# Weight sums on VectorE, a tap and roundings on ScalarE, and stored split weights for the short MLP

## The chip, the core and the metric

The kernel runs on one core of one Trainium2 chip. The metric is the device time of one execution in microseconds.

## The reference

One encoder layer is applied to two sequences with shared weights: `x_sample` (1024 positions, the long one, done first) and `x_prompt` (512, the short one). D_MODEL is 1024, D_FF 3072. Only the second half of the layer matters here:

```python
mix = (sigmoid(gate_lru) * y_lru + sigmoid(gate_attn) * y_attn) @ w_o + b_o
x = layer_norm(ALPHA * x + mix, ln1_g, ln1_b)
hu = depthwise_conv(x @ w_up + b_up, w_ffn_conv, b_ffn_conv, (1, 1))
val, gt = split(hu, 2)
ffn = (gelu(gt) * val) @ w_down + b_down
return layer_norm(ALPHA * x + ffn, ln2_g, ln2_b)
```

Before it stand a projection, a bidirectional gated recurrence (RG-LRU) and a windowed attention. All is float32.

## The kernel before, in words

**Split products.** Every matrix product is made of float32r pieces: a value is rounded to a head, and the tail is the value less the head. Head x head, head x tail and tail x head are summed, so a product takes three matmuls per tile. For weights, the head is a copy (`tensor_scalar` by 1, or a ScalarE copy) into an F32R tile and the tail a `tensor_tensor` subtraction.

**Order.** Phases are `lru`, `attn` (with its output projections `y_lru`, `y_attn`, `w_o`) and `mlp`, first for the long sequence (q = 0), then for the short one (q = 1). In `lru` to `w_o` of the long sequence GpSimd splits each weight slab (L939, L940), SyncE (SP) stores the split slab in the DRAM array `w_split` (L715), and the short sequence reads it back (`fetch`, L718 to L721). The MLP's weights were not stored: the short sequence loaded them raw (`short_slab`, L912 on) and GpSimd split them again (`split_short`, L1099, the rounding L1106 and the subtraction L1107).

**Engines.** Each engine runs its own written-out list of instructions in order, tied to the others by semaphores whose counts are constants or, in loops, register values (`Fori`, `order.loop`). `order(...)` and `tell(...)` on VectorE make every instruction wait for the one before it.

**Long MLP, up.** A feature tile p (128 of 3072) has a value row and a gate row of 1024 positions, `lv_raw` and `lg_raw`. Two tiles (PLAIN) are computed plainly, with split slabs `plain`. The other 22 (FAST) are computed as pairs of 2x2 block products in Winograd's form: seven products instead of eight, `form_product` (L1533), 12 matmuls of 128x512 each. The weight side needs three plain blocks A11, A12, A22 and four sums S1 to S4, each as head and tail of 128x512 (`forms`). GpSimd makes the sums (`pair_forms`: L1036, L1038, L1043, L1044) and all seven tails (L1050), ScalarE the heads (`round_plain_forms` L2078, `round_sums` L2083). The products go in the order A11, S2, S1, A12, S3, S4, A22 into three PSUM banks of `FORM_BANKS[side]`; a bank is taken by VectorE between two products into it: `gate_second` (L2626) before S3, `value_second` (L2632) before S4, the value half of `second_halves` (L2639) before A22, the gate half (L2641) after it, and `value_first` (L2619) when the pair is done. ScalarE takes two more (`first_product` L2090, `gate_half` L2097).

The depthwise convolution of tile p = j + 1 runs beside pair j: for the gate, ScalarE does the centre tap with the bias (`centre`, L2063) and VectorE the two outer ones (L2591, L2594), then ScalarE the gelu (L2068); for the value VectorE does all three (L2599, L2601, L2603). `hidden` (L2611) multiplies them to `l_h`, which SP stores in `h_dram` (`store_h`). A raw pair of slabs is loaded by `load_pair` on SP once `form_done` says that the former pair's tiles are read (L820).

**Long MLP, down.** 48 steps: 24 k-tiles for four token tiles, then the same 24 for the other four. A step has 24 matmuls (L1588). Per step SP loads a raw slab of `w_down` (128x1024) and a half row of `h_dram` (128x512); GpSimd splits the slab (`down_slab`, L1075, L1076) into one of four ring slots `W_down`, and VectorE splits the hidden tile (`split_down_h`, L2655, L2656). Beside it VectorE prepares the residual (`start_long_sum`, L2663, L2665), and ScalarE issues the loads of `acc_down` (4 MB), of the next x (2 MB) and of five row vectors. After each half, `last_sum` and the layer norm of its token tiles run on VectorE and ScalarE.

**Short MLP.** Six groups of 12 slabs: eight up slabs (four pairs of value and gate tiles) and four down slabs, 24 matmuls each. ScalarE takes the up results from PSUM (L2158), VectorE does six taps, the product with the gelu, the cast and the tail (L2553 to L2566), and TensorE then runs the down slabs (L1483). The 12 slabs rotate over five buffers:

```python
UP_SLOT = (4, 0, 1, 2, 3, 4, 1, 4)
DOWN_SLOT = (0, 2, 3, 1)
```

so slab 7 goes where slab 5 was, and slab 2 where slab 11 of the group before was.

## Time and profile before

| | |
|---|---|
| median of three runs | 2790.64 us (2790.28 to 2797.62) |
| the profiled execution | 2797.58 us |
| its span, first to last instruction | 2795.8 us |
| mean granted TensorE clock | 0.974 |
| TensorE busy | 2642.1 us (95%) |
| VectorE busy | 1710.3 us (61%) |
| GpSimd busy | 1259.0 us (45%) |
| ScalarE busy | 848.8 us (30%) |
| DMA | 452.77 MB, mean 162 GB/s |
| chain that ended last | TensorE 62%, VectorE 16%, GpSimd 12%, ScalarE 4%, DMA 3% |

The span is the time between the first and the last instruction of the one execution that was profiled, and some 1.8 us of its time lie around it. The shares are of the span. The chain is followed back from the last instruction, at each step to what released it; an engine with a large share there held the others up. In rows of a timeline, brackets name the idle time before an instruction and what ended it.

### The profile page before, as it was taken

Reading aid. Unit: us, or ns where it says so; the run is one execution under the profiler, and the core shown is the slowest. Engines: PE = TensorE matmul, PEld = TensorE weight load, DVE = VectorE, ACT = ScalarE, POOL = GpSimd, SP = SyncE. Lnnn points to the kernel's source line nnn. Section 1 sums busy time; section 2 is a strip of 40 time slices with the busy share of each in tenths; the row PEclk is TensorE's granted clock in tenths of the full one; section 3 lists DMA queues with packets and bytes.
Section 4 is the critical chain, followed back from the end, with each engine's and each line's share of the span. In section 5 each row is a group of like instructions: output and inputs, shape, how many; then the busy total and the mean of one; then the engine's idle time right before and its main releaser. Section 6 shows DMA issues by size and latency. Waiting matters only on the chain.

```text
span 2795.8 us, 33187 instructions
## 1 busy us (share of the span) xinstructions
PE 2642.1 (95%) x11634; PEld 2166.8 (78%) x11634; DVE 1710.3 (61%) x1883; ACT 848.8 (30%) x1224; POOL 1259.0 (45%) x680
## 2 busy tenths in 40 slices
PE   8998999999899999999999798999999898899997
...
GB/s 220 194 189 160 205 172 143 192 158 159 246 341 241 284 92 46 87 71 82 75 81 129 219 137 152 169 211 226 217 222 196 330 238 76 79 87 90 90 88 85
DMA packets 155869, 452.77 MB, mean 162 GB/s; under 512 B 13895, under 2 KB 40775, under 8 KB 153712
## 3 DMA queue, kind: packets, MB, share of 16 engines
...
## 4 chain that ended last, share of the span: by engine, by line
PE 62%; DVE 16%; POOL 12%; ACT 4%; DMA 3%; issue 2%; ACTq 0%; SPq 0%; POOLq 0%; DVEq 0%
PE ps L1139 31%; PE ps L1309 8%; PE ps L1588 7%; POOL S L1050 6%; PE ps L1403 4%; POOL A L1050 3%; PE ps L1191 3%; PE ps L1483 2%; PE ps L1292 2%; PE ps L1342 1%; POOL S_sum L1036 1%; DMA gate_in<-gate_dram 1%; DVE HL L2566 1%; PE ps L1329 1%; PE ps L1194 1%
## 5 line engine op out<-in xcount | busy, mean ns | idle before, releaser
L1139 PE MATMUL ps<-XH,W 128*128 128x512 f32 x2752 | 811.3, 393 | 24.4 <-DVE XL L2244 11.9
L1139 PEld LDWEIGHTS ps<-XH,W 128*128 128x128 f32 x2752 | 519.8, 189 | 141.3 <-issue 17.7
L1139 PE MATMUL ps<-XL,W 128*128 128x512 f32 x1376 | 484.6, 392 | 0.0
L1106 POOL TENSOR_SCALAR W<-raw 128x1024 fp32r<-128x1024 f32 x72 | 83.3, 1157 | 677.7 <-PE ps L1403 502.7
L939 POOL TENSOR_SCALAR W<-raw 128x1024 fp32r<-128x1024 f32 (+2 forms) x72 | 91.8, 1275 | 567.2 <-PE ps L1139 301.8
L1139 PEld LDWEIGHTS ps<-XL,W 128*128 128x128 f32 x1376 | 260.6, 189 | 54.2
L1588 PE MATMUL ps<-Wd,Hd 128*128 128x512 f32 x1152 | 271.9, 399 | 26.7 <-DVE Hd L2656 23.5
L1588 PEld LDWEIGHTS ps<-Wd,Hd 128*128 128x128 f32 x1152 | 222.3, 194 | 76.2 <-issue 20.1
L1309 PE MATMUL ps<-XH,W 128*128 128x512 f32 x672 | 216.4, 393 | 0.0
L940 POOL TENSOR_TENSOR W<-raw,W 128x1024 fp32r<-128x1024 f32 (+2 forms) x72 | 206.5, 2868 | 6.0
L1533 PE MATMUL ps<-XH,A 128*128 128x512 f32 x528 | 173.4, 396 | 16.7 <-DVE lv_raw L2639 13.1
L1107 POOL TENSOR_TENSOR W<-raw,W 128x1024 fp32r<-128x1024 f32 x72 | 183.9, 2555 | 6.0
L1050 POOL TENSOR_TENSOR S<-S_sum,S 128x512 fp32r<-128x512 f32 x88 | 174.3, 1981 | 13.8 <-POOL S L1050 9.5
L1309 PEld LDWEIGHTS ps<-XH,W 128*128 128x128 f32 x672 | 126.2, 188 | 25.5
L1483 PE MATMUL ps<-W,HH 128*128 128x512 f32 x384 | 115.2, 420 | 28.7 <-DVE HL L2566 16.5
L1533 PEld LDWEIGHTS ps<-XH,A 128*128 128x128 f32 x528 | 99.9, 189 | 45.6 <-DVE lv_raw L2639 19.9
L1309 PE MATMUL ps<-XL,W 128*128 128x512 f32 x336 | 131.1, 390 | 0.0
L1076 POOL TENSOR_TENSOR Wd<-raw,Wd 128x1024 fp32r<-128x1024 f32 x48 | 124.9, 2603 | 4.0
L2655 DVE CAST Hd<-Hd 128x512 fp32r<-128x512 f32 x48 | 50.0, 1041 | 109.1 <-DMA Hd<-h_dram 108.1
L1483 PEld LDWEIGHTS ps<-W,HH 128*128 128x128 f32 x384 | 78.1, 205 | 48.3 <-ACT v_raw L2158 12.7
L1050 POOL TENSOR_TENSOR A<-raw,A 128x512 fp32r<-128x512 f32 x66 | 104.1, 1577 | 10.8 <-POOL A L1050 6.3
L1139 PE MATMUL ps<-ATH,W 128*128 128x512 f32 x384 | 108.2, 389 | 0.0
...
## 6 DMA issues: line engine op xcount, KB each, us to landing
w_split<-W SPq DMA_DIRECT2D x59, 1024.0 KB, 6.0
W<-w_split SPq DMA_DIRECT2D x58, 1024.0 KB, 5.6
...
```

The source lines that it names most:

```text
L939: order(pool.tensor_scalar(half(0, slot, 0)[:, 0:width], raw[slot][:, 0:width], 1.0, 1.0, ALU.mult, ALU.mult))
L940: return pool.tensor_tensor(half(0, slot, 1)[:, 0:width], raw[slot][:, 0:width], half(0, slot, 0)[:, 0:width].bitcast(F32), ALU.subtract)
L1050: pool.tensor_tensor(F[n][:, 1, :], src, F[n][:, 0, :].bitcast(F32), ALU.subtract).then_inc(form_done, 1)
L1076: pool.tensor_tensor(tail, raw[k % 2][:, 0:D_MODEL], head.bitcast(F32), ALU.subtract).then_inc(wd_split, 1)
L1107: pool.tensor_tensor(tail, raw[n % 2][:, 0:D_MODEL], head.bitcast(F32), ALU.subtract).then_inc(short_split, 1)
L1139: last = nc.tensor.matmul(bank(group, c), lhs(wl, k), rhs(xl, k, c), start=(k == 0 and n == 0), stop=(k == nk - 1 and n == 2))
L1191: nc.tensor.matmul(ps[:, first + c, :], w[wl][:, m * P:(m + 1) * P], ut[xl][:, c * CH:(c + 1) * CH], start=(i == 0), stop=False)
L1309: last = nc.tensor.matmul(ps[:, 2 + side, :], half(q, slot_of(q, "attn", slab), wl)[:, k * P:(k + 1) * P], x_rhs(xl, k, c), start=(k == 0 ...
L1403: last = nc.tensor.matmul(ps[:, 2 * pair + f, :], X[q][xl][:, k, tt * P:(tt + 1) * P], half(q, slot_of(q, "w_o", k), wl)[:, f * CH:(f + 1) ...
L1483: last = nc.tensor.matmul(ps[:, 2 * pair + f, :], (HH, HL)[xl][:, kk, tt * P:(tt + 1) * P], half(q, DOWN_SLOT[kk], wl)[:, f * CH:(f + 1) * ...
L1533: last = nc.tensor.matmul(ps[:, bank_no, :], forms[side][form][:, wl, k * P:(k + 1) * P], x_form(of, xl)[:, k, :], start=(start and k == 0 ...
L1588: last = nc.tensor.matmul(ps[:, first + f, :], H_down[slot][:, xl, (tt % 4) * P:(tt % 4 + 1) * P], W_down[slot][:, wl, f * CH:(f + 1) * CH ...
```

## The change

- **Weight sums and their tails.** S1 to S4 and their four tails are made by VectorE (`first_sums`, `last_sums`, `split_sums`), spread over its `pair_period`. GpSimd keeps the tails of A11, A12 and A22 (`split_plain_forms`).
- **A tap.** The value's centre tap with the bias goes to ScalarE (`value_centre`); VectorE keeps two value taps.
- **Down.** ScalarE rounds the weight slab and the hidden tile (`round_step`), VectorE subtracts both (`split_step`), one signal `step_split` for the two. `start_long_sum` is spread, one token tile a step, over steps 8 to 15.
- **Stores.** SP stores the split plain slabs, the three split plain forms of each pair (three times 512 KB) and, in the first half of down, each split `w_down` slab (1 MB). The fourth block A21 was never split for the long sequence: in the down-phase SP loads it raw (`rest_raw`, 256 KB), GpSimd splits it, SP stores it (512 KB), 22 times. Ring slots and forms wait for their stores.
- **Short MLP.** SP fetches split slabs (1 MB) straight into the five buffers; GpSimd does nothing there.

The core of the diff:

```diff
+                def save_forms(j, side, slab):
+
+                    sp.wait_ge(a_split, 3 * j + 3)
+                    for n in PLAIN_TILES:
+                        at = slice(0, CH) if n[2] == "1" else slice(CH, 2 * CH)
+                        sp.dma_start(w_split[slab + (n[1] == "1"), :, :, at],
+                                     forms[side][n][:, :, :].bitcast(F32)).then_inc(form_saved[side][0], 16)
+
+                def next_pair(j, side, slab):
+                    save_forms(j - 1, side, slab)
+                    sp.wait_ge(form_added, 4 * j)
                     load_pair(j + PLAIN)
                     store_h(j - 1)
...
+                def save_down(kk, slot, slab):
+                    sp.wait_ge(step_split, kk + 1)
+                    sp.dma_start(w_split[slab, :, :, 0:D_MODEL], W_down[slot][:, :, :].bitcast(F32)).then_inc(w_saved[slot], 16)
+
+                def load_rest(i, slab, k):
+                    sp.dma_start(rest_raw[k][:, :], A["w_up"][slab, :, 0:CH]).then_inc(rest_in[k][0], 16)
+
+                def save_rest(i, slab, k):
+                    sp.wait_ge(rest_split, i + 1)
+                    sp.dma_start(w_split[slab, :, :, 0:CH], rest[k][:, :, :].bitcast(F32)).then_inc(rest_saved[k][0], 16)
...
+                for kk in range(RING, FT):
+                    next_step(kk, kk, 0, kk % RING)
+                    save_down(kk - RING, kk % RING, down_slab(kk - RING))
+                    i = kk - RING
+                    if i >= 2:
+                        sp.wait_ge(rest_split, i - 1)
+                    load_rest(i, 2 * (PLAIN + i), i % 2)
+                    if i:
+                        save_rest(i - 1, up_slab(PLAIN + i - 1, 0), (i - 1) % 2)
...
-                    sp.wait_ge(out_stored[k], 16 * out_count(0)[k])
+                s0 = first_slab(1, "mlp")
                 for n in range(12):
-                    if n >= 2:
-                        sp.wait_ge(short_split, n - 1)
-                    sp.dma_start(raw[n % 2][:, 0:D_MODEL], short_slab(0, n)).then_inc(raw_in[n % 2], 16)
+                    if n == 1:
+
+                        sp.wait_ge(res_taken[1], T // P - 2)
+                    if n == 2:
+                        sp.wait_ge(res_taken[1], T // P)
+                    first_use = SLOT[n] not in SLOT[:n]
+                    fetch(s0 + (2 if first_use and n > 2 else 3 - SLABS["w_o"] if first_use else n - slot_user(n) + 3),
+                          FIRST["mlp"] + n, SLOT[n])
...
+                    def split_plain_forms(j, side):
+
+                        for i, n in enumerate(PLAIN_TILES):
                             pool.wait_ge(form_rounded, 7 * j + i + 1)
-                            src = weight_raw(n) if n[0] == "A" else low[n]
-                            pool.tensor_tensor(F[n][:, 1, :], src, F[n][:, 0, :].bitcast(F32), ALU.subtract).then_inc(form_done, 1)
-                            pool.wait_ge(form_done, 7 * j + i + 1)
-
-                    def split_t3():
-                        pool.wait_ge(t_rounded, 3)
-                        pool.tensor_tensor(XT[2][1][:, :, :], t_sum[2][:, :, :], XT[2][0][:, :, :].bitcast(F32),
-                                           ALU.subtract).then_inc(t3_split, 1)
-
-                    pair_forms(0, 0, split_t3)
-                    pair_forms(1, 1)
+                            pool.tensor_tensor(forms[side][n][:, 1, :], weight_raw(n), forms[side][n][:, 0, :].bitcast(F32),
+                                               ALU.subtract).then_inc(a_split, 1)
+                            pool.wait_ge(a_split, 3 * j + i + 1)
...
+                        def value_centre(p):
+
+                            if isinstance(p, int) and p < PLAIN:
+                                act.wait_ge(up_evac[0], 2 * p + 2)
+                            else:
+                                act.wait_ge(form_taken, 5 * p - 5)
+                            if not (isinstance(p, int) and p == 0):
+                                act.wait_ge(h_ready, p)
+                            A1(lv_conv[:, :], lv_raw[:, 1:T + 1], ACT.Identity, scale=col("fconv_w", 2 * FT + p),
+                               bias=col("fconv_b", p)).then_inc(conv_begun[0], 1)
...
+                        def pair_period(j, side, saved=0, ahead=True):
+                            p = j + PLAIN - 1
+                            if ahead:
+                                round_plain_forms(j + 1, 1 - side, saved)
+                            value_centre(p)
                             first_product(j, side)
+                            gelu(p)
                             if ahead:
-                                round_plain_forms(j + 1, 1 - side)
-                            gelu(j + PLAIN - 1)
-                            if ahead:
-                                round_sums(j + 1, 1 - side)
+                                round_sums(j + 1, 1 - side, DONE_ORDER[3:5])
+                                round_sums(j + 1, 1 - side, DONE_ORDER[5:7])
                             gate_half(j, side)
-                            centre(j + PLAIN)
+                            gate_centre(p + 1)
...
+                        def round_step(s):
+
+                            k, slot = s % 2, s % RING
+                            act.wait_ge(raw_in[k], 16 * (RAW_DOWN + s // 2 + 1))
+                            if s < 2:
+                                act.wait_ge(form_used, 7 * FAST - 7)
+                                act.wait_ge(form_saved[0][0], FORM_BASE + 24 * FAST)
+                            elif s < RING:
+                                act.wait_ge(form_used, 7 * FAST if s == 3 else 7 * FAST - 4)
+                            else:
+                                act.wait_ge(step_used, s - 3)
+                                act.wait_ge(w_saved[slot], 16 * (TOTAL[0][slot] + min(s, FT + RING - 1) // RING))
+                            A1(W_down[slot][:, 0, :], raw[k][:, 0:D_MODEL], ACT.Copy).then_inc(down_rounded, 1)
+                            act.wait_ge(h_landed[slot][0], H_BASE + 16 * (s // RING + 1))
+                            A1(H_down[slot][:, 0, :], H_down[slot][:, 1, :].bitcast(F32), ACT.Copy).then_inc(down_rounded, 1)
...
+                    def first_sums(j, side):
+
+                        total = form_sum[side]
+                        for k in range(2):
+                            dve.wait_ge(raw_in[k], 16 * (RAW_UP + PLAIN) + 16 * j + 16)
+                        wait_pair_slots(dve, j)
+                        tell(V.tensor_tensor(total["S1"][:, :], weight_raw("A21"), weight_raw("A22"), ALU.add), form_added, 4 * j + 1)
+                        tell(V.tensor_tensor(total["S2"][:, :], total["S1"][:, :], weight_raw("A11"), ALU.subtract), form_added, 4 * j + 2)
+
+                    def last_sums(j, side):
+
+                        total = form_sum[side]
+                        if isinstance(j, int) and j < 2:
+
+                            dve.wait_ge(slab_done, s0 + 4)
+                            dve.wait_ge(plain_saved, 16 * 4 * PLAIN)
+                        tell(V.tensor_tensor(total["S3"][:, :], weight_raw("A11"), weight_raw("A21"), ALU.subtract), form_added, 4 * j + 3)
+                        tell(V.tensor_tensor(total["S4"][:, :], weight_raw("A12"), total["S2"][:, :], ALU.subtract), form_added, 4 * j + 4)
+
+                    def split_sums(j, side, at):
+
+                        for i in at:
+                            n = DONE_ORDER[3 + i]
+                            dve.wait_ge(form_rounded, 7 * j + 4 + i)
+                            tell(V.tensor_tensor(forms[side][n][:, 1, :], form_sum[side][n][:, :], forms[side][n][:, 0, :].bitcast(F32),
+                                                 ALU.subtract), s_split, 4 * j + i + 1)
+
+                    def pair_period(j, side, ahead=True):
 
                         p = j + PLAIN - 1
-                        gate_taps(p, lambda: value_first(j - 1, 1 - side))
-                        value_taps(p, lambda: gate_second(j, side))
-                        value_second(j, side)
+                        if not (isinstance(j, int) and j == 0):
+                            value_first(j - 1, 1 - side)
+                        gate_taps(p)
+                        if ahead and not (isinstance(j, int) and j == 0):
+                            first_sums(j + 1, 1 - side)
+                        value_taps(p)
+                        gate_second(j, side)
+                        if isinstance(j, int) and j == 0:
+                            value_second(j, side)
+                            dve.wait_ge(t_rounded, 4)
+                            tell(V.tensor_tensor(x_form("T4", 1), x1b[:, half_k:KD, :], x_form("T4", 0).bitcast(F32), ALU.subtract),
+                                 t_split, 3)
+                            first_sums(j + 1, 1 - side)
+                            last_sums(j + 1, 1 - side)
+                        else:
+                            if ahead:
+                                last_sums(j + 1, 1 - side)
+                            value_second(j, side)
                         hidden(p)
-                        second_halves(j, side)
-
-                    def split_down_h(s, s4, slot):
-
-                        dve.wait_ge(h_landed[slot], 16 * s4 + 16)
-                        order(V.tensor_copy(H_down[slot][:, 0, :], H_down[slot][:, 1, :].bitcast(F32)))
+                        if ahead:
+                            split_sums(j + 1, 1 - side, (0, 1))
+                        value_third(j, side)
+                        if ahead:
+                            split_sums(j + 1, 1 - side, (2, 3))
+                        gate_third(j, side)
...
+                    def split_step(s):
+
+                        k, slot = s % 2, s % RING
+                        dve.wait_ge(down_rounded, 2 * s + 1)
+                        order(V.tensor_tensor(W_down[slot][:, 1, :], raw[k][:, 0:D_MODEL], W_down[slot][:, 0, :].bitcast(F32), ALU.subtract))
+                        dve.wait_ge(down_rounded, 2 * s + 2)
                         tell(V.tensor_tensor(H_down[slot][:, 1, :], H_down[slot][:, 1, :].bitcast(F32),
-                                             H_down[slot][:, 0, :].bitcast(F32), ALU.subtract), h_split[0], s + 1)
+                                             H_down[slot][:, 0, :].bitcast(F32), ALU.subtract), step_split, s + 1)
```

In VectorE's up-phase the loop now covers pairs 2 to 19 (`order.loop(FAST // 2 - 2, 6)`); pairs 0, 1, 20 and 21 are written out. On VectorE `split_step` of steps 25 to 27 now stands between the sums of the first token tiles.

## Rows read from the trace of the kernel before

**Rows 1.** Stretch of the long up-phase; each engine busy us (instructions), clock, DMA share, GB/s.

```profile
1180.00:1500.00 320.00, 309.20 (x1343) 249.74 (x1342) 221.50 (x176) 115.63 (x176) 291.49 (x176) 1.00 0.24 79
```

**Rows 2.** The chain that ended last: start us, us, what.

```profile
757.21 168.91 PE ps L1139 x744
...
1500.14 19.38 PE ps L1533 x84
```

**Rows 3.** TensorE's timeline, 1500 to 1710 us: start, us, what, idle before in brackets.

```profile
1528.03 20.95 PE L1588 MATMUL ps<-Wd,Hd 128*128 128x512 f32 x84 [3.02 <-DVE lv_raw L2619]
1558.60 23.76 PE L1588 MATMUL ps<-Wd,Hd 128*128 128x512 f32 x96 [9.63 <-DVE Hd L2656]
1587.18 94.13 PE L1588 MATMUL ps<-Wd,Hd 128*128 128x512 f32 x402 [4.82 <-DVE Hd L2656]
...
1699.35 10.91 PE L1588 MATMUL ps<-Wd,Hd 128*128 128x512 f32 x41 [6.66 <-DVE Hd L2656]
```

**Rows 4.** Stretches of the short MLP, columns as in rows 1.

```profile
2428.60:2500.30 71.70, 68.61 (x289) 55.92 (x289) 51.44 (x41) 10.29 (x14) 44.19 (x24) 0.95 0.28 89
2711.90:2795.00 83.10, 68.03 (x288) 55.29 (x288) 60.93 (x61) 17.75 (x27) 36.38 (x20) 0.91 0.26 89
```

**Rows 5.** The chain in the short MLP.

```profile
2350.26 4.73 PE ps L1472 x27
...
2428.66 32.94 PE ps L1139 x144
...
2491.70 8.47 PE ps L1483 x24
...
2769.59 15.98 PE ps L1483 x60
```

**Rows 6.** VectorE's timeline in the short MLP.

```profile
2452.12 0.75 DVE L2555 SCALAR_TENSOR_TENSOR v_conv<-v_raw,cols,v_conv 128x512 f32<-128x512 f32 x1
...
2463.29 2.66 DVE L2555 SCALAR_TENSOR_TENSOR g_conv<-g_raw,cols,g_conv 128x512 f32<-128x512 f32 x1
```

**Rows 7.** GpSimd's timeline at the same place.

```profile
2462.92 2.48 POOL L1107 TENSOR_TENSOR W<-raw,W 128x1024 fp32r<-128x1024 f32 x1
```

**Rows 8.** VectorE's timeline in a loop pair of the long up-phase.

```profile
1302.06 1.90 DVE L2591 SCALAR_TENSOR_TENSOR lg_conv<-lg_raw,cols,lg_conv 128x1024 f32<-128x1024 f32 x1 [1.58 <-ACT lg_conv L2063]
...
1304.98 1.28 DVE L2594 SCALAR_TENSOR_TENSOR lg_conv<-lg_raw,cols,lg_conv 128x1024 f32<-128x1024 f32 x1
1306.46 1.51 DVE L2599 TENSOR_SCALAR lv_conv<-lv_raw,cols 128x1024 f32<-128x1024 f32 x1 [0.19 <-DVE lg_conv L2594]
1308.22 0.69 DVE L2626 TENSOR_TENSOR lg_raw<-ps,l_e 128x512 f32<-128x512 f32 x1 [0.25 <-PE ps L1533]
1309.06 1.29 DVE L2601 SCALAR_TENSOR_TENSOR lv_conv<-lv_raw,cols,lv_conv 128x1024 f32<-128x1024 f32 x1 [0.15 <-DVE lg_raw L2626]
```

**Rows 9.** VectorE's timeline outside the loop, GpSimd idle.

```profile
1019.55 0.69 DVE L2522 TENSOR_TENSOR XL<-x,XH 128x512 fp32r<-128x512 f32 x1
...
1083.82 1.28 DVE L2601 SCALAR_TENSOR_TENSOR lv_conv<-lv_raw,cols,lv_conv 128x1024 f32<-128x1024 f32 x1
1085.14 1.28 DVE L2603 SCALAR_TENSOR_TENSOR lv_conv<-lv_raw,cols,lv_conv 128x1024 f32<-128x1024 f32 x1
...
1537.30 1.22 DVE L2611 TENSOR_TENSOR l_h<-lv_conv,lg_conv 128x1024 f32<-128x1024 f32 x1
```

**Rows 10.** GpSimd's timeline in the pair of rows 8.

```profile
1303.04 2.08 POOL L1050 TENSOR_TENSOR S<-S_sum,S 128x512 fp32r<-128x512 f32 x1 [0.16 <-POOL A L1050]
```

**Rows 11.** DMA view of 1546-1560, 2205-2222 and 941-957 us; the last row: whole run.

```profile
DMA packets 1627, 5.42 MB, mean 387 GB/s; under 512 B 177, under 2 KB 177, under 8 KB 1627
...
DMA packets 2206, 6.83 MB, mean 402 GB/s; under 512 B 157, under 2 KB 157, under 8 KB 2071
...
DMA packets 1299, 4.93 MB, mean 308 GB/s; under 512 B 99, under 2 KB 99, under 8 KB 1298
...
W<-w_split SPq DMA_DIRECT2D x58, 1024.0 KB, 5.6
```

335 lines of the change are left out of this document (169 added, 166 removed).

## The prediction

> **What bounds the kernel now.** I read the page first (busy shares, the chain that ended last), then stretches with the busy time of each engine, then the chain and the timelines inside the long and the short MLP, and last the DMA view. The change touches three stretches: the long up-phase (about 1046 to 1520 us), the long down-phase (to about 1820) and the short MLP (2340 to the end).
>
> Up-phase: between 1180 and 1500 us there are 16 pairs of feature tiles, 20.03 us each. TensorE is busy 309.2 of 320 us, but VectorE only 221.5 and GpSimd 291.5 [rows 1]. The last 84 matmuls of a pair take 19.4 us when nothing is missing [rows 2], so about 0.8 us of each pair is waiting, and GpSimd, with 11 instructions in a pair and 18.2 us busy, is what the loop waits for.
>
> Down-phase: 48 steps of 24 matmuls, 5.45 us each (744 in a row take 168.9 us, so 0.227 each [rows 2]). From 1519.5 us to step 28 the 28 steps need 152.6 us and get 192, because TensorE stands still 3.0, 9.6, 4.8 and 6.7 us, and the matmuls just behind each stop are slow [rows 3]: 12 matmuls lie before the first of these rows and 30 ahead of the last, so 26 steps are done at 1699.4, and the next two end at 1711.5.
>
> Short MLP: a group of 288 matmuls needs 65.4 us (288 x 0.227), and the four middle ones take 283.3 together, 71.7 for the first, with a granted clock of 0.95 [rows 4]: near the upper of the two levels, 2.4 GHz, with dips after stops. 24 matmuls behind a stop took 8.47 us instead of 5.45 [rows 5]. The stop is VectorE's: the same instruction that takes 0.75 us at 2452 takes 2.66 at 2463, while GpSimd's 2.48 us subtraction runs beside it [rows 6, 7].
>
> **What GpSimd and VectorE do to each other.** In a loop pair, the tap of 1302.06 takes 1.90 us; the same kind of instruction takes 1.28 us with GpSimd idle. GpSimd's subtraction of 1303.04 takes 2.08 us and ends 1.16 us after that tap [rows 8 to 10]. So they take turns on instructions with two SBUF operands. Reads of PSUM stay at 0.69 (1308.22) [rows 8]. The Trainium skill ("SBUF — State Buffer", Who interferes with whom) says that the pair shares a port as an exclusive lock, and that a VectorE instruction with one SBUF operand outside the two-port modes is not touched; the trace agrees, with 0.69 us for a PSUM read in a stretch where GpSimd is 91% busy [rows 1, 8].
>
> **1. Up-phase, the period of a pair.** Removed from GpSimd: four sums and four of seven remainders; three remain. ScalarE gets a centre tap (some 1.25 us; it was busy 115.6 of 320 us [rows 1], so it has room). VectorE loses one tap and gets four sums and four remainders of 128x512: 18 instructions. Durations: tap 1.28, two-SBUF instruction of 512 columns 0.69, of 1024 columns 1.22 [rows 9]; PSUM read 0.69 [rows 8]. Work alone: 4 taps 5.12 + hidden 1.22 + 8 x 0.69 + 5 x 0.69 = 15.3 us. That would be well under 19.2. But two things come on top.
> - Gaps. In the loop the steps between VectorE's instructions are 0.20, 0.25 and 0.15 us [rows 8]; in code written out, 0.04 [rows 9]. I take 0.16, near the lowest in the loop.
> - GpSimd's three remainders start when ScalarE has rounded, which waits for the end of pair j-1, just when VectorE begins its own period. VectorE is never idle then, so each costs it 0.6 (the 1.90 above) to 1.16 us (a whole turn); I take 0.8.
> - The last product of a pair (A22) waits for value_third, and value_first of the next period waits for A22. So the loop is: 15 of the 18 instructions (13.2 us; the last two remainders and gate_third lie beside A22), 14 gaps (2.2), three turns (2.4), A22 itself (2.7), two handovers (0.2): **20.8 us**, against 20.03. VectorE takes GpSimd's place as the bound and is 0.8 us worse. In the same sum, gate_second would come at about 11.7 us, where TensorE wants it at 10.9: another sign that VectorE is late.
>
> 18 of the 22 pairs are in the loop: +14. Pairs 20 and 21 are written out on VectorE (0.04 gaps) and fall to TensorE's 19.2: -1.6. At the start GpSimd no longer competes with VectorE's long subtractions: -2. Sum **+11 us**. Bounds: with gaps 0.04 and turns 0.6 the loop is 18.5, TensorE binds at 19.2, and the phase gains 19; with gaps 0.20 and turns 1.16 it is 22.5 and loses 41.
>
> The saves of forms, 1.5 MB in a pair beside 1.5 MB moved before, make 3.1 MB in 20 us, or 150 GB/s; the stretch moved 79 and the queue reaches 387 [rows 11], so they hide. They stand on SP ahead of the pair's load: the save waits for GpSimd's third remainder (at about 7 us), the load for the last sum (about 13 us), lands about 4 us later, and is wanted at 21. The eight saves of the plain slabs (4.2 MB, 11 us at 387 GB/s, from 1030) are done before ScalarE rounds the first forms, after 1060. If DMA were busy there, the first pair would be late by as much.
>
> **2. Down-phase.** GpSimd's rounding and subtraction go to ScalarE (128x1024 and 128x512) and VectorE (1.22 + 0.69 us): under 2.5 us of a 5.45 us step, hidden. A step also waits for its ring slot to be saved. The new cost is DMA. Before, a step moved 0.79 MB (weights 0.52, hidden 0.26). In the first half it now moves also the split slab (1.05 MB), a raw quarter (0.26) and its split (0.52): 2.62 MB. Full queues moved 387 and 402 GB/s [rows 11]; at 400 a step takes 6.55 us, above TensorE's 5.45. TensorE starts step 4 about 35 us after the phase begins (39 before: VectorE's taps there no longer wait for GpSimd, but the 6.3 MB of ScalarE's loads still stand before the step's own), then 24 steps at 6.55 are 157, and the output stores (2.1 MB) 5 more: 198 against 192, say **+7**. The stop in the middle (6.7 us, VectorE with stretched instructions) goes, but the transfers fill the room. Bounds: if DMA never held a step back, 28 steps would be near 165, or -27; at 308 GB/s, the rate of a stretch that SP's queue had nearly alone [rows 11], 8.5 us a step, or +54. The remaining 20 steps are at TensorE's pace in both.
>
> **3. Short MLP.** Raw loads, 12 roundings and 12 subtractions a group (44 us of GpSimd in 71.7 [rows 4]) go; SP reads a split slab (1 MB) instead. 12 MB in 66 us are 190 GB/s, hidden. VectorE then has every instruction at its short length: a pair of taps, product, cast and remainder is about 7.7 us against TensorE's 10.9 for its two slabs, and the last remainder comes 6 us behind the last up slab, where TensorE wants it after 16. So the stop and the slow matmuls behind it go. New wait: slab 7 of a group uses the buffer that slab 5 just left, with one slab of 5.45 us between; a read takes 5.6 us to land [rows 11] plus the issue, so I count 0.7 us a group. A group becomes 66.1: four middle ones give 283.3 - 264.4 = 19 us. The last group and its tail take 83.1 us [rows 4]. Its last matmul ends at 2785.6 [rows 5], 73.7 us after the group's start for 65.4 of work: 8 go, the tail stays. The first: TensorE passes 2355 (the chain's 4.73 us from 2350.26) with 54.5 us of work before 2428.66 [rows 5], 73.7 us; with 3 us of waits left, -16. Sum -43; I take **-42**. Bounds: -30 (half the first and last gains stay) to -48.
>
> **Sum.** +11 + 7 - 42 = -24 us. The profiled execution took 2797.6 us (span 2795.8 and 1.8 around it), so it would take about 2773.6. Its time lies 7 above the median of the runs, 2790.6; the median is then forecast at **2766 us**.
>
> **Rivals.**
> - VectorE doesn't bind the up-phase (gaps hidden behind the instructions): it gains 19 instead of losing 11, total -54, 2737 us. For: 18 instructions are only 15.3 us. Against: the gaps were 0.15 to 0.25 in every loop row shown. 0.18.
> - Slower: the down-phase saves hold TensorE. If the queue gives 308 GB/s, its first half costs 54 instead of 7, total +23, 2814 us. It decides against the change above 7.5 us a step, so below 348 GB/s. For: SP issues these transfers in order, between waits, so the queue runs empty. Against: 387 and 402 with both queues. 0.15.
> - VectorE binds harder (22.5 us a pair): total +6, 2797 us. 0.12.
> - Slab 7's read lands as late as some reads beside other traffic, 10 us: 4.5 us in six groups, total +3, 2794 us. 0.07.
> - Reads and writes together run slower than the reads of the two fast stretches: halfway between 387 and 308 GB/s is 348, or 7.5 us a step, 23 us more than forecast; total -1, 2789 us. The fast stretches are mostly reads, which is for it. 0.05. The Trainium skill ("DMA: Bandwidth & Descriptors", Where 436 GB/s comes from) has a rule that speaks for this rival: memory's share for a core binds a transfer at about 358 GB/s. By that rule, and as an estimate, a step would be 7.3 us and the total -6. The rows of 387 and 402 GB/s are above it [rows 11].
> - The short MLP keeps its stops, for VectorE's own length is the cause: no gain there, total +18, 2809 us. Against: 0.75 beside 2.66 us [rows 6]. 0.03.
>
> The forecast's own case has 0.40. A change of 0.3% is 8.4 us, about what measuring can tell from none. Faster: nearly all of the forecast's case (0.38), the first rival (0.18) and the low ends of the others: 0.60. Same 0.20: the third, fourth and fifth in most of their spread. Slower 0.20: the second, the sixth and the rest. The range, 2738 to 2800, leaves out one in ten at each end.
>
> **What will show it.** Pairs in the loop 20.8 us apart, with TensorE waiting for value_third (VectorE) and GpSimd busy some 4 to 6 us a pair; steps of the first down half 6.5 us apart, DMA share near 1 there, the second half 5.45; groups of the short MLP near 66 us with a clock of 1.00, GpSimd idle, VectorE's taps all at 0.75. Pairs at 19.2, steps at 5.45 or above 7.5, or groups still at 70 would each show a term wrong.

## The result, and the profile after

The changed kernel takes 2815.97 us (median of three, 2814.96 to 2816.67) against 2790.64: a ratio of 1.0082, 95% interval 1.0058 to 1.0107. It is slower, and outside the range of 2738 to 2800: I had forecast 2766 and given slower two chances in ten. The profiled execution took 2814.96 us (span 2812.9), 17 us more than the one before; the two spans are the ones that the ledger below divides up.

| where (by the spans) | forecast | measured | from |
|---|---|---|---|
| up-phase, to its last matmul | +11 | +23.5 | it ends at 1545.8 in place of 1522.2 us |
| down-phase, to its last matmul | +7 | +48 | the next sequence's first matmul starts at 1892.1 in place of 1820.5 |
| short sequence | -42 | -54.5 | the rest, up to +17.1 at the end |

All three have the forecast's sign. The short sequence paid for the change, and the two long phases lost it again and 17 us beside it.

The table holds one execution against one, and that of the kernel before was 7 us above its median; the medians lie 25.3 us apart, not 17.1. A second profile of nearly the same code shows where the 8 us are: the kernel before with one loop written out (its run is below, 2789.17 us). From the first matmul of w_o in the short sequence to the end it took 503.8 us in place of 513.4, and its down-phase was 3.5 us shorter; the changed kernel took 459.3 for the former. Against this profile that stretch gains 44.5 us, not 54.1. And recurrence and attention of the short sequence, where all kernels of this document run the same code, took 461.0 to 467.6 us in 14 profiles: a row of such a table is good to a few microseconds only.

**Up-phase.** The stretch that answers to [rows 1], columns as there:

```profile
1180.00:1500.00 320.00, 297.11 (x1270) 236.16 (x1271) 271.96 (x274) 130.19 (x183) 88.03 (x45) 1.00 0.41 149
```

GpSimd has gone from 291.5 to 88.0 us, VectorE from 221.5 to 272.0, and TensorE does less in the same time: 15 pairs in place of 16. Loop pairs come alternately 21.04 and 21.27 us apart, 21.16 in the mean. What TensorE waits for there (waits of PE in the same stretch: us in total, times, longest):

```profile
PE ps L1541 <- DVE lg_raw L2685: 17.3, 16, 1.2
PE ps L1541 <- DVE lv_raw L2697: 6.4, 15, 0.5
```

L2685 is gate_second, L2697 value_third. One pair on VectorE, cut to what I read from it:

```profile
1297.80 2.09 DVE L2654 SCALAR_TENSOR_TENSOR lg_conv<-lg_raw,cols,lg_conv 128x1024 f32<-128x1024 f32 x1
1300.20 1.40 DVE L2712 TENSOR_TENSOR S_sum<-raw 128x512 f32<-128x512 f32 x1 [0.31 <-DVE lg_conv L2654]
1301.63 1.67 DVE L2713 TENSOR_TENSOR S_sum<-S_sum,raw 128x512 f32<-128x512 f32 x1
1303.54 1.28 DVE L2660 SCALAR_TENSOR_TENSOR lv_conv<-lv_raw,cols,lv_conv 128x1024 f32<-128x1024 f32 x1 [0.24 <-DVE S_sum L2713]
1304.97 1.28 DVE L2662 SCALAR_TENSOR_TENSOR lv_conv<-lv_raw,cols,lv_conv 128x1024 f32<-128x1024 f32 x1 [0.15 <-DVE lv_conv L2660]
1306.50 0.69 DVE L2685 TENSOR_TENSOR lg_raw<-ps,l_e 128x512 f32<-128x512 f32 x1 [0.25 <-DVE lv_conv L2662]
```

Three instructions are long, by 0.81, 0.71 and 0.98 us over what their like take alone [rows 9]: GpSimd's three turns, 2.5 us. The gaps of the loop are there too, up to 0.31 us; with those under 0.5 us alone they come to 2.3 us a pair.

**Down-phase.** TensorE's timeline, as in [rows 3]:

```profile
1584.94 13.44 PE L1598 MATMUL ps<-Wd,Hd 128*128 128x512 f32 x48 [13.01 <-DVE Hd L2768]
1602.94 7.37 PE L1598 MATMUL ps<-Wd,Hd 128*128 128x512 f32 x24 [4.56 <-DVE Hd L2768]
1611.62 5.74 PE L1598 MATMUL ps<-Wd,Hd 128*128 128x512 f32 x24 [1.31 <-DVE Hd L2768]
1618.19 5.74 PE L1598 MATMUL ps<-Wd,Hd 128*128 128x512 f32 x24 [0.83 <-DVE Hd L2768]
...
1715.92 2.83 PE L1598 MATMUL ps<-Wd,Hd 128*128 128x512 f32 x6 [5.17 <-DVE Hd L2768]
1722.56 16.84 PE L1598 MATMUL ps<-Wd,Hd 128*128 128x512 f32 x66 [3.81 <-DVE Hd L2768]
1746.46 2.92 PE L1598 MATMUL ps<-Wd,Hd 128*128 128x512 f32 x6 [7.07 <-DVE small L2873]
1756.11 2.93 PE L1598 MATMUL ps<-Wd,Hd 128*128 128x512 f32 x6 [6.72 <-DVE small L2873]
1763.88 36.34 PE L1598 MATMUL ps<-Wd,Hd 128*128 128x512 f32 x152 [4.84 <-DVE small L2873]
```

Three things are to be seen. Step 4 starts after a stop of 13 us. Then TensorE stops ahead of nearly every step: from 1618.2 to 1722.6 fifteen steps take 104.4 us, 6.96 each. (In the runs below a step is the time from one split on VectorE to the next, over the same fifteen steps, 8 to 23.) And in the middle there is not one stop of 6.7 us [rows 3] but five of 3.8 to 7.1 us, with single tiles of 6 matmuls between them that take 2.9 us (1.65 at full pace): the granted clock was 0.60 in the mean of 1740 to 1770 us, so mostly at the lower of its two levels, 1.2 GHz. Before the first two of the five, VectorE's split of the next step is missing, before the other three its sum over a finished bank (L2873). DMA from 1600 to 1700 us:

```profile
DMA packets 14138, 37.92 MB, mean 379 GB/s; under 512 B 1163, under 2 KB 1163, under 8 KB 14135
```

**Short sequence.** The chain, as in [rows 5]:

```profile
2516.62 21.76 PE ps L1491 x96
2538.52 32.94 PE ps L1149 x144
2571.62 5.34 DMA W<-w_split
2577.01 5.78 PE ps L1149 x24
2582.79 21.76 PE ps L1491 x96
```

A group is now 66.1 us (2516.62 to 2582.79 from one row of 96 down matmuls to the next) in place of 70.8, its matmuls at 0.227 to 0.229 us each. The read of slab 7 (5.34 us here) starts when slab 5's matmuls end, and lands just as slab 6's do: it costs next to nothing. GpSimd does nothing, and none of VectorE's taps is lengthened (0.75 us each, 0.55 for the first of each three).

### The profile page after: what moved, and what is told of

Its sections match the earlier page's. It is cut to its first block, busy times and chain, and to the rows that moved or that the text cites. A ratio compares the mean times of both kernels' runs of the same rounds, so it can differ in the third digit from the quotient of the medians.

```text
span 2812.9 us, 32874 instructions
## 1 busy us (share of the span) xinstructions
PE 2634.9 (94%) x11634; PEld 2150.6 (76%) x11634; DVE 1642.0 (58%) x2035; ACT 959.0 (34%) x1344; POOL 591.6 (21%) x308
## 4 chain that ended last, share of the span: by engine, by line
PE 67%; DVE 19%; DMA 6%; ACT 3%; issue 2%; SPq 1%; POOL 1%; DVEq 1%; ACTq 0%; POOLq 0%
PE ps L1149 33%; PE ps L1317 8%; PE ps L1598 5%; PE ps L1491 5%; PE ps L1411 4%; PE ps L1541 4%; DMA rest_raw<-w_up 3%; PE ps L1199 2%; PE ps L1300 2%; DVE lg_conv L2654 2%; PE ps L1350 1%; DVE S_sum L2713 1%; DVE lg_conv L2652 1%; DVE S_sum L2712 1%; DVE lv_conv L2660 1%
## 5 line engine op out<-in xcount | busy, mean ns | idle before, releaser
L1149 PE MATMUL ps<-XH,W 128*128 128x512 f32 x2752 | 812.1, 393 | 25.1 <-DVE XL L2305 11.7
L1598 PE MATMUL ps<-Wd,Hd 128*128 128x512 f32 x1152 | 282.0, 406 | 64.4 <-DVE Hd L2768 45.8
L1149 PEld LDWEIGHTS ps<-XL,W 128*128 128x128 f32 x1376 | 260.5, 189 | 54.1
L1092 POOL TENSOR_TENSOR A<-raw,A 128x512 fp32r<-128x512 f32 x66 | 126.3, 1914 | 329.2 <-ACT A L2103 322.6
L2766 DVE TENSOR_TENSOR Wd<-raw,Wd 128x1024 fp32r<-128x1024 f32 x48 | 60.4, 1259 | 139.3 <-ACT Wd L2176 139.1
L2176 ACT ACTIVATE Wd<-raw 128x1024 fp32r<-128x1024 f32 x48 | 50.8, 1059 | 189.3 <-DMA w_split<-Wd 152.8
L1957 ACT ACTIVATE gate_in<-gate_in 128x1024 f32<-128x1024 f32 (+1 forms) x32 | 26.9, 846 | 241.3 <-DMA gate_in<-gate_dram 241.2
L1903 ACT ACTIVATE probs<-probs,small 128x384 f32<-128x384 f32 (+1 forms) x96 | 54.5, 569 | 157.1 <-DVE small L2464 157.1
L1541 PE MATMUL ps<-XL,A 128*128 128x512 f32 x264 | 104.1, 394 | 0.0
L1491 PE MATMUL ps<-W,HH 128*128 128x512 f32 x384 | 103.6, 389 | 0.0
L1199 PE MATMUL ps<-u_head,W 128*128 128x512 f32 x240 | 83.9, 404 | 17.4 <-ACT sig L1788 16.3
```

Source lines behind the costliest of these rows:

```text
L1092: pool.tensor_tensor(forms[side][n][:, 1, :], weight_raw(n), forms[side][n][:, 0, :].bitcast(F32), ALU.subtract).then_inc(a_split, 1)
L1149: last = nc.tensor.matmul(bank(group, c), lhs(wl, k), rhs(xl, k, c), start=(k == 0 and n == 0), stop=(k == nk - 1 and n == 2))
L1199: nc.tensor.matmul(ps[:, first + c, :], w[wl][:, m * P:(m + 1) * P], ut[xl][:, c * CH:(c + 1) * CH], start=(i == 0), stop=False)
L1491: last = nc.tensor.matmul(ps[:, 2 * pair + f, :], (HH, HL)[xl][:, kk, tt * P:(tt + 1) * P], half(q, DOWN_SLOT[kk], wl)[:, f * CH:(f + 1) * ...
L1541: last = nc.tensor.matmul(ps[:, bank_no, :], forms[side][form][:, wl, k * P:(k + 1) * P], x_form(of, xl)[:, k, :], start=(start and k == 0 ...
L1598: last = nc.tensor.matmul(ps[:, first + f, :], H_down[slot][:, xl, (tt % 4) * P:(tt % 4 + 1) * P], W_down[slot][:, wl, f * CH:(f + 1) * CH ...
```

## The experiments

Each time stands beside runs of the kernel before on the same chip; the ratios are to those. What a run gains over the changed kernel is counted from that kernel's three executions (2815.97 us), which were not repeated beside it, so 2 or 3 us are within what sets of runs differ by: the medians of the kernel before were 2789.3 to 2792.3. Timeline numbers are of each kernel's own profile.

### VectorE's loop, written out

```
-                        with order.loop(FAST // 2 - 2, 6) as i:
-                            for k in range(2):
-                                pair_period(2 * i + 2 + k, k)
-                        pair_period(FAST - 2, 0)
+                        for j in range(2, FAST - 1):
+                            pair_period(j, j % 2)
```

> The changed kernel, with VectorE's loop over the pairs of the up-phase written out (its waits are then on constants), nothing else changed; GpSimd, ScalarE and TensorE keep theirs. Theory A (VectorE sets the pair, and a good part of its time is the gap of 0.15 to 0.25 us between two of its instructions that waits against a register's value leave in the loop): 18 gaps a pair fall from a mean of 0.16 to 0.04 us, 2.2 us a pair, more than the 1.8 us by which the pair (21.16 us) is longer than TensorE's 84 matmuls (19.36 us), so the pairs come at 19.4 to 19.7 us: 20 pairs by 1.5 to 1.8 us, 30 to 35 us less, 2781 to 2786 us. Rival B (the pair is set by the chain between the engines, form sum to rounding to remainder and the turns with GpSimd, not by VectorE's own time): pairs stay within 0.3 us of 21.16, and the time within 6 us of 2816. Rival C (the written-out instructions have to be loaded and stall VectorE): pairs longer than 21.2 us, slower than 2816.

2798.0 us (10 runs), 18.0 under the changed kernel; against the kernel before 1.0024 [1.0013, 1.0035]. Pairs come 20.02 us apart, every one of them. So VectorE was the bound and its gaps were most of it: rivals B and C fall, but the gain is 1.14 us a pair, not 1.5 to 1.8, and the time is 12 us above the range. The rest shows in VectorE's timeline:

```profile
1306.79 0.75 DVE L2678 SCALAR_TENSOR_TENSOR lv_raw<-ps,small,l_e 128x512 f32<-128x512 f32 x1 [1.06 <-PE ps L1541]
1307.58 1.28 DVE L2652 SCALAR_TENSOR_TENSOR lg_conv<-lg_raw,cols,lg_conv 128x1024 f32<-128x1024 f32 x1
1308.90 2.20 DVE L2654 SCALAR_TENSOR_TENSOR lg_conv<-lg_raw,cols,lg_conv 128x1024 f32<-128x1024 f32 x1
1311.13 1.67 DVE L2712 TENSOR_TENSOR S_sum<-raw 128x512 f32<-128x512 f32 x1
1312.84 1.66 DVE L2713 TENSOR_TENSOR S_sum<-S_sum,raw 128x512 f32<-128x512 f32 x1
...
1317.17 0.69 DVE L2685 TENSOR_TENSOR lg_raw<-ps,l_e 128x512 f32<-128x512 f32 x1
```

VectorE now waits 1.06 us a pair for TensorE, so it isn't full. But gate_second still ends 11.1 us after value_first began, and TensorE wants it then: the order of VectorE's work costs 0.37 us a pair. The step between two instructions is 0.04 us everywhere, and GpSimd's three turns are whole ones now, 0.92 + 0.98 + 0.97 = 2.9 us. That closes the account of a pair: the gaps fell by 1.75 us (2.32 to 0.57), the turns took 0.4 of it back, and the wait for TensorE 0.25.

### The same in the kernel before

The loop of the kernel before, written out in the same way.

> The kernel before with VectorE's pair loop written out, nothing else. In it VectorE stands idle 3.0 and 1.6 us a pair behind ScalarE, so by theory A (the written-out loop pays where VectorE sets the pair) it gains little: 0 to 4 us, from the shorter way of gate_second and value_third on TensorE's waits. Rival (the loop gap costs either kernel the same): 15 to 20 us faster, 2770 to 2776 us.

2790.39 us against 2792.34, ratio 1.0001 [0.9987, 1.0015]: no difference. The pairs went from 20.03 to some 19.96 us. Here VectorE waits 3.0 and 1.6 us a pair for ScalarE, so the gaps cost next to nothing; the written-out loop is worth 18 us only with what the change put on VectorE.

### The sums back on GpSimd

```
                     def split_plain_forms(j, side):
+                        pool.tensor_tensor(total["S1"][:, :], weight_raw("A21"), weight_raw("A22"), ALU.add).then_inc(form_added, 1)
+                        ...
+                        pool.tensor_tensor(total["S4"][:, :], weight_raw("A12"), total["S2"][:, :], ALU.subtract).then_inc(form_added, 1)
...
-                            first_sums(j + 1, 1 - side)
...
-                                last_sums(j + 1, 1 - side)
```

> The changed kernel with the four sums of each pair back on GpSimd (seven GpSimd operations a pair in place of three); their remainders stay on VectorE, whose loop is a loop again. Theory X (a turn of GpSimd on operands in SBUF costs VectorE about what its own 128x512 operation does: 2.9 us a pair for three turns in the written-out loop, 0.96 each, against 0.69 and a gap of 0.16): VectorE loses 4 by 0.85 us and gains 4 by 0.96 us a pair, the pair is 21.2 to 21.9 us, the time 2814 to 2830 us. Rival Y (the move of the sums is what made the up-phase longer): pair at 20.0 to 20.4 us, as before the change, and the time 2790 to 2800 us.

2856.61 us, ratio 1.0237 [1.0217, 1.0258]: 41 us slower than the changed kernel, pairs 22.7 us apart. Rival Y falls. Theory X has the sign and not the size (its range ended at 2830), since its sum over VectorE's time left out what stood behind the sums. Waits of VectorE, 1180 to 1500 us:

```profile
DVE lv_conv L2676 <- ACT lv_conv L2099: 61.0, 14, 4.7
```

VectorE, with its sums gone, waits 4.4 us a pair for ScalarE's centre tap, which stands behind the three roundings of the weights, and these behind the weights' landing. The value taps start 8.3 us after value_first here and 8.2 in the changed kernel (1303.70 and 1303.54): the sums had filled a wait. Then GpSimd's seven turns fall on the taps (2.1 us each in place of 1.28) and push gate_second back. So with the rest of the change as it is, the sums are better on VectorE, and they cost less there than their own length. No run puts the four remainders or the centre tap back by themselves, so what each of these costs is not known.

### The rests left out

The reads, splits and stores of the 22 rests are gone; the short sequence reads other slabs of the same size in their place.

> The changed kernel without the 22 rests of w_up in the down-phase (neither read, nor split on GpSimd, nor stored; the short MLP reads the value slabs of pair 0 in their place, so the second output is not the reference's, with transfers of the same size). The stores of W_down stay. Theory D (the first half of the down-phase is bound by the bytes of SP's queue, 2.62 MB a step with the rests and 1.83 MB without): at the measured 379 GB/s 1.83 MB take 4.8 us, under TensorE's 5.53 us, so the step falls from 6.9 to 5.6 us, and the stop of 13 us before step 4 shrinks by about 2 us: 20 steps by 1.3 us and 2 us, 28 us less, and up to 10 us more if the stops in the middle go as well: 2778 to 2788 us. Rival E (the step is set by the four slots of the weights, which are rounded, used, and stored before the next use, whatever else is in the queue): the step stays at 6.5 us or more, and the time above 2805 us.

2794.71 us, 21 under the changed kernel (1.0008 [0.9997, 1.0019] to the one before). Expected were 28 to 38 (theory D) or at most 11 (rival E). The step fell from 6.96 to 6.09 us, not to 5.6: neither theory. The chain of waits between 1631 and 1657 us says what holds it:

```profile
1631.15 0.33 SPq L857
1631.52 0.43 SPq L860
1632.00 7.85 DMA w_split<-Wd
...
1639.95 1.07 ACT Wd L2148
...
1641.11 1.24 DVE Wd L2738
1642.37 1.67 DVE Hd L2740
1644.06 0.33 SPq L857
```

From one read that SP issues to the next on this chain it is 12.9 us, and that is two steps. SP issues the read for step s+2 when step s is split, and only behind it the store of step s-2, which lands in 7.85 us and lets ScalarE round step s+2 (four slots). The queue was not full: 0.85 of DMA's time, 300 GB/s. So there is a second limit of 6.1 to 6.5 us just below the first.

### Three slots for the rests

```
-                    load_rest(i, 2 * (PLAIN + i), i % 2)
-                    if i:
-                        save_rest(i - 1, up_slab(PLAIN + i - 1, 0), (i - 1) % 2)
+                    load_rest(i, 2 * (PLAIN + i), i % 3)
+                    if i >= 2:
+                        save_rest(i - 2, up_slab(PLAIN + i - 2, 0), (i - 2) % 3)
```

> The changed kernel with three slots for the rests in place of two, and SP storing rest i-2 in the step in which it reads rest i, so that SP no longer waits for a rest that it issued one step ago; bytes and instructions are the same. Theory D (bytes of the queue): nothing moves, step 6.8 to 7.0 us, 2810 to 2820 us. Rival F (SP's own wait sets the step: a rest's read lands 8.0 us after its issue, GpSimd takes 0.64 and 2.11 us and waits between, SP then issues its store, and two slots over that round trip of some 13.6 us are 6.8 us a step): with three slots the step falls to what the queue gives at its best slices (410 to 420 GB/s for 2.62 MB, 6.3 us), 24 steps by 0.5 us, 2800 to 2806 us.

2809.2 us, 6.8 less. Steps of 6.37 us, at 405 GB/s from 1620 to 1700 us where the changed kernel moved 374. The same bytes went faster, so the rate was not the engines' own: SP had stood waiting for rests. The step comes out as rival F had it (6.3 us); the total is 3 us above its range, and theory D's time, 2810, is as near. It is the step and the rate that decide for F.

### The rests in the second half

```
+                    if kk:
+                        i = kk - 1
+                        load_rest(i, 2 * (PLAIN + i), i % 2)
+                        ...
                 with sp.Fori(0, FT // RING - 2) as i:
                     for k in range(RING):
                         next_step(RING * i + FT + RING + k, RING * i + RING + k, 1, k)
+                        late_rest(RING * i + 3 + k, i, k)
```

> The changed kernel with the 22 rests moved from steps 4 to 27 of the down-phase to steps 25 to 47, where SP's queue carries 0.79 MB a step; GpSimd makes the eight remainders of the next sequence's input before the rests in place of after them. Theory D (bytes): first half as without the rests (step 5.6 us), second half 1.57 MB a step at 379 GB/s or more is 4.1 us, below TensorE's 5.53 us, so it stays hidden: 26 to 38 us less, 2778 to 2790 us. Rival G (GpSimd's turns hold up VectorE's remainder of H, 1.60 us where it takes 0.69 us alone, in whichever half the rests are, and that sets the step): the second half's steps grow by 0.5 us or more (20 by 0.5 are 10 us) and the whole gains under 20 us.

2795.43 us, 20.5 less, 1.0017 [1.0007, 1.0026]. The first half is about as without the rests (5.90 us a step), and the second hides them: TensorE runs without a stop of over 1 us from 1740.6 us to the end of the phase, though GpSimd and VectorE are both at work. Rival G falls. The time is 5 us above the range, for the reason found above: the ring of the stores takes over.

### The stores two steps earlier

```
                     load_down(kk, k % 2)
+                    if isinstance(s, int) and s < FT + 2:
+                        save_down(s - 2, (s - 2) % RING, down_slab(s - 2))
...
-                    save_down(kk - RING, kk % RING, down_slab(kk - RING))
```

> The changed kernel with SP issuing the store of W_down's halves for step s-2, right behind the read of step s, in place of the store for step s-4 behind H's read; bytes, rests and all other instructions are the same. Theory H (the step without the rests, 6.45 us, is a ring on SP: the remainder of H of step s lets SP read for step s+2, only then the store of step s-2 is issued, lands in 7.8 us, and lets ScalarE round step s+2, so two steps take 0.76 + 7.8 + 1.1 + 1.2 + 1.7 us and the gaps): with the rests still there the bytes bind next, 2.62 MB at the 405 GB/s of the run with three slots are 6.5 us a step against 6.95, some 20 steps by 0.45 are 9 us; step 4's halves start after their read (issued 1567.9) and no store, 5 us earlier; the stops in the middle 3 to 5 us less: 2797 us, 2792 to 2802. Rival D (bytes alone, at 379 GB/s, whatever the order): 2810 us or more.

2813.27 us (2812.55 to 2815.31), 2.7 less, which is not clear of the spread, where I had counted on 19. By its time alone this is rival D's run (2810 or more); what speaks against D is the run with three slots, where the same bytes went faster, and the trace. Steps are 6.79 us. Its chain from 1600 us on has turned into the rests:

```profile
1638.67 7.29 DMA rest_raw<-w_up
1646.14 1.15 POOL rest L1116
1647.36 2.15 POOL rest L1117
1649.53 5.74 DMA w_split<-rest
1655.34 2.14 POOL rest L1117
1657.50 4.08 DMA w_split<-rest
```

With two slots for the rests this ring holds the step as well as the other did. Step 4 did start earlier (a stop of 7.2 us in place of 13.0), but stops of 3.4 and 7.9 us at steps 5 and 6 gave that back.

### Three of the down-phase's edits together

Three slots, earlier stores, and the middle in its old order (below), with the rests where the change puts them.

> The changed kernel with the rests where they are, and three of the edits of the down-phase together: three slots for the rests, W_down's stores two steps earlier, the middle in its old order. Theory R (two rings on SP, that of the rests and that of the stores, and the bytes lie close together, so that each edit alone shows the next of them): only the bytes stay, 2.62 MB at 405 GB/s, 6.5 us a step; against the changed kernel 8 us for the steps, 3 to 5 us for step 4's start, 9 to 12 us in the middle: 2791 to 2797 us. Rival D (bytes alone at 379 GB/s set the first half): only the middle moves, 2803 to 2807 us.

2789.98 us (8 runs), 1.0002 [0.9992, 1.0013]: 26 us under the changed kernel, as much as the kernel before. Steps of 6.36 us at 414 GB/s. This is 1 us beyond the range, on theory R's side: rival D falls. But the step is the one that three slots alone gave (6.37), so the earlier stores add nothing to it here. From step 8, which starts at 1618.2 us as in the changed kernel, to step 23 it took 8.9 us less, and from there to where 28 steps are done 44.4 us in place of 60.5: 16 of the 26 us are the middle's.

DMA from 1600 to 1700 us, to be held against 37.92 MB above:

```profile
DMA packets 15346, 41.39 MB, mean 414 GB/s; under 512 B 1278, under 2 KB 1278, under 8 KB 15342
```

The DMA engines had read as full in the changed kernel as well, and yet 9% more bytes fit into the same time once SP no longer waited for the rests (7% more with three slots alone).

### Loop, late rests and earlier stores; then the middle

Three edits at once, and the same with the middle's order turned back:

> Three edits at once: VectorE's pair loop written out (20 us in its own run), the rests in the second half (22 us in its own run), and the stores of W_down two steps earlier. Theory H: with the rests out of the first half and the ring gone, the step of the first half is TensorE's 5.53 us (1.83 MB at 400 GB/s are 4.6 us), 20 steps by 0.8 us less than in the run with late rests alone, the start of step 4 5 us and the middle 3 us earlier: 2795 - 20 - 16 - 8 = 2751 us, 2745 to 2758. Rival D (bytes alone): the late rests have taken all there was, 2772 to 2778 us.

> The kernel of the three edits with, beside them, the order in the middle of the down-phase as the kernel before had it: VectorE takes the sums of tiles 1, 2 and 3 before it splits steps 25 to 27, and ScalarE rounds those steps after the square of tile 1. Theory M (the stops in the middle, some 23 us in all with late rests, are the order: the sums that empty the banks stand behind the splits of steps 25 to 27, whose slots come free only with the end of the first half): 8 to 14 us less than the kernel of three edits. Rival N (the stops are the stores and reads of steps 24 to 27 and stay, only the place changes): within 4 us of it.

```
+                        if tt + 1 < nt and not (q == 0 and tt == 3):
+                            last_sum(tt + 1)
+                        if q == 0 and tt == 2:
+                            for s in range(FT + 1, FT + 4):
+                                split_step(s)
-                        if q == 0 and tt < 3:
-                            split_step(FT + 1 + tt)
```

The first: 2759.84 us, 0.9885 [0.9858, 0.9911], 2 us outside its range and far from rival D. The second: 2747.21 us, 0.9844 [0.9819, 0.9869]. The order in the middle is worth 12.6 us, as theory M had it (8 to 14). TensorE's timeline, first without it, then with it:

```profile
1670.42 17.64 PE L1604 MATMUL ps<-Wd,Hd 128*128 128x512 f32 x66 [3.66 <-DVE Hd L2774]
1689.35 1.66 PE L1604 MATMUL ps<-Wd,Hd 128*128 128x512 f32 x6 [1.29 <-DVE small L2877]
1697.20 2.93 PE L1604 MATMUL ps<-Wd,Hd 128*128 128x512 f32 x6 [6.19 <-DVE small L2877]
1704.51 55.76 PE L1604 MATMUL ps<-Wd,Hd 128*128 128x512 f32 x234 [4.38 <-DVE small L2877]
```

```profile
1670.30 37.46 PE L1604 MATMUL ps<-Wd,Hd 128*128 128x512 f32 x156 [3.10 <-DVE Hd L2775]
1710.80 49.53 PE L1604 MATMUL ps<-Wd,Hd 128*128 128x512 f32 x210 [3.04 <-DVE Hd L2775]
```

The cause of it in the changed kernel: TensorE may enter a bank of the second half when VectorE has taken its sum. But VectorE first splits steps 25 to 27, each of which needs ScalarE's rounding, and that a slot which comes free only when the last tile of the first half is done and its store has landed. ScalarE waited 13.8 us for a store there, and VectorE 11.0 us for ScalarE.

### Two sums of the up-phase earlier

gate_second moved ahead of the value taps, value_third ahead of the four remainders, on top of all that:

```
+                            gate_second(j, side)
                         value_taps(p)
-                        gate_second(j, side)
...
+                        value_third(j, side)
                         if ahead:
-                            split_sums(j + 1, 1 - side, (0, 1))
-                        value_third(j, side)
+                            split_sums(j + 1, 1 - side, range(4))
```

> The kernel of the four edits (VectorE's loop written out, late rests, earlier stores, the middle in its old order), and beside them VectorE takes gate_second ahead of the two value taps, and value_third right behind the product of value and gate, ahead of all four remainders of the sums. Theory A (in the written-out loop VectorE's chain from one pair's A22 to gate_second is 11.2 us against the 11.1 us of the four products before S3, which leaves TensorE 0.37 us of waiting a pair, and its chain to value_third 16.8 us against 16.6 us for the six products before A22): with both moved up the pair falls from 20.02 to 19.4 to 19.6 us, TensorE's own 19.36: 18 to 20 pairs by 0.4 to 0.6 us, 8 to 12 us less than that kernel, 2735 to 2740 us. Rival O (VectorE's sum of 18.9 us a pair and the delayed centre tap or gelu take over): the pair stays above 19.9 us, within 3 us.

2738.27 us, 0.9815 [0.9799, 0.9831], 9 us less. Pairs 19.69 us apart; gate_second and value_third have gone from TensorE's waits, and value_second (L2698, 0.35 us a pair) has taken their place. Rival O falls, but it has a grain of truth: each wait removed shows a smaller one.

### ScalarE's reads behind the start of the down-phase

```
+                        for s in (4, 5):
+                            round_step(s)
                         for tt in range(nt):
                             act.dma_start(acc_down[:, tt, :], z1_dram[tt, :, :])
-                        for s in (4, 5):
-                            round_step(s)
```

A wait of ScalarE ahead of those reads (for `t_rounded`) is left out with it.

> The kernel of the run just above, with the eight reads of the residual sum (4 MB on ScalarE's queue) issued behind the rounding of steps 4 and 5 in place of ahead of it. Theory S (the stop before step 4, 7.8 us here, is the read and the store of H's last tiles standing in the DMA engines behind 6 MB of ScalarE's reads): the stop falls by 3 to 5 us and the time with it. Rival T (it is the row of waits on SP, the last product on VectorE at the end of the up-phase, its store, the wait for it and only then step 4's reads): within 1.5 us of it, or later stops give it back.

2734.82 us (2733.59 to 2738.75), 0.9799 [0.9783, 0.9816]. The median is 3.5 us under the run above, but the ranges of the two overlap, and the profiles speak against theory S: the stop before step 4 fell only from 5.7 to 4.8 us, a new one of 4.1 us came at 1583.7, and the phase ended at 1814.1 us in place of 1809.6. Whether this edit gains anything stays open. Either way, the last two kernels beat both the changed kernel and the one before.

## Why the prediction was wrong

**Short sequence: right in its mechanism, 12 us too small.** The stops were GpSimd's, as I had read from [rows 6, 7]: groups of 66.1 us, as forecast; the four middle groups gave 18.9 us (19) and the last with its tail 7.8 (8). In the first group the six remaining up slabs and the four down slabs took 55.1 us in place of 71.0 (from 2417.4 to 2472.5, before from 2357.7 to 2428.7): 15.9 us, where I had 16 (counted from 2355). The 12 us that I had not counted lie ahead of that. From the first matmul of w_o to the last of the MLP's first two slabs it took 63.8 us in place of 75.3, and I had not looked there because no line of the change stands in it. But GpSimd had split the MLP's first weights there too, beside VectorE's layer norm and split of x. One cast in the kernel before with GpSimd beside it, and its like in the changed kernel:

```profile
2321.65 2.37 POOL L1107 TENSOR_TENSOR W<-raw,W 128x1024 fp32r<-128x1024 f32 x1
2322.14 2.02 DVE L2521 CAST XH<-x 128x256 fp32r<-128x256 f32 x1 [1.83 <-ACT x L2019]
...
2392.17 0.29 DVE L2582 CAST XH<-x 128x256 fp32r<-128x256 f32 x1 [1.83 <-ACT x L2028]
```

Six VectorE instructions between 2318 and 2349 us are longer in this way, by 7.8 us together, each under an instruction of GpSimd. So GpSimd's turns fall on casts with one operand as well, and not only on instructions with two, which is all that I had read from [rows 8 to 10]. No run was made on this stretch alone, but the 12 profiles of kernels with the stored weights show w_o's first matmul to the MLP's first 47.0 us apart, and the two without 51.9 and 50.0.

**From the profile to the median: 7 us taken off twice.** I took the stops to be removed from an execution that lay 7 us above its median, and then took 7 us off once more to get at the median. As far as the one other profile shows, the excess lay in the stretch whose stops the change removes (513.4 us against 503.8), so these 7 us were in my gain already. They are most of the 8 us between the table's +17 and the medians' +25.

**Up-phase: +23.5 for +11.** The bound was named rightly (VectorE), and its price was mis-sized. The term was "20.8 us" a pair and came out at 21.16; the 18 pairs of the loop took 18.5 us more than before, where I had 14. Turns (2.5 us against my 2.4) and gaps were as counted, but I closed the loop over value_third and A22 and took gate_second, "at about 11.7 us, where TensorE wants it at 10.9", only as "another sign". Of TensorE's 1.5 us of waits a pair, 1.08 are there, and with both moved up the pair fell to 19.69. The larger part is the start. I had "-2" for it; the first matmul of the pairs came 4.8 us earlier, but the first pair then took 34.9 us where it had taken 25.9, with stops of 2.2 us for VectorE's first remainder, 6.0 for ScalarE's l_e (3.5 before) and 3.4 ahead of A22, and the second pair took 1.0 more: +5.2 in all. The last one ends with value_third (done at 1101.29 us, A22 starts at 1101.39), and in this pair VectorE had the tail of T4 (2.3 us), four sums, the product and two remainders ahead of it. No run was made on the start. The lower bound that I gave (TensorE binding at 19.2) was reached by no run: the written-out loop gave 20.02, and 19.69 with two sums moved.

**Down-phase: +48 for +7.** This is the step that failed: the terms for the middle, the step and the start were each too small. By these three it came out 42 us longer than forecast. (The sum itself was rounded up: 35, 157 and 5 are 197, so +5, which I put down as +7.)
- "The stop in the middle (6.7 us) goes, but the transfers fill the room." It became five stops. From 1722.6 us, the last step of the first half, to where 28 steps are done (1783, counting back 20 steps from the end of the phase) it took 60 us; my 6.55 a step and 5 for the stores make 38: 22 us. I had read in the diff that rounding moves to ScalarE and had asked only what it takes (under 2.5 us), not what it waits for and who stands behind it. The run with the order turned back gave 12.6 us, and with the rests in the first half, as here, the middle is 16 us shorter.
- "At 400 a step takes 6.55 us." The rate was a good guess: with all rings out of the way the same bytes ran at 414 GB/s and 6.36 us a step. But the changed kernel ran at 6.96, 6 us over fifteen steps, since SP issues its transfers one by one behind waits. The ring of the rests is slower than the bytes (three slots alone brought 6.37), and that of the stores lies close to them (6.1 to 6.5 where the rests are gone). I had written of just this, in the rival of slower saves ("SP issues these transfers in order, between waits, so the queue runs empty"), and gave it a threshold of 7.5 us a step with 0.15. The time came out where that rival has it (2814), by another sum: no step reached 7.5 us in the mean.
- "TensorE starts step 4 about 35 us after the phase begins": 41.8, with another 7 us in the four steps behind it. Issuing the stores earlier brought step 4 forward by 5 to 7 us, but step 8 then started no earlier than before (1618.2 us with all three edits). What holds the steps between stays open.

The two rivals that hung on the rate alone fall with it. None of the long mixed stretches ran at 348 GB/s: it was 379, 405 and 414 over 80 to 100 us. The Trainium skill has two statements on this. "DMA: Bandwidth & Descriptors" (Where 436 GB/s comes from) lets some 358 GB/s bind every transfer between memory and SBUF, and these stretches contradict it. "Perfetto Trace Analysis" (Roofline) calls the same figure a share that counts when both cores of a pair are active, and sets the limit of a single one some 120% of it, about 430; with one busy core and 414 GB/s, the trace agrees with that.

What the change does, taken together, is well chosen, and what it lost was order: its own arithmetic with five edits of order beside it is 2738 us, 1.8% under the kernel before. By the profiles nearly all of that is the short sequence's (45 of 52 us, against the kernel before with its loop written out, the profile near the median); the down-phase starts 3 us earlier and is 4 us shorter. What each edit is worth alone doesn't quite add up: three slots 6.8 us, earlier stores 2.7, old middle order 12.6 on another base, 22 in all, and 26 together.
